# Scales of the Strassen pairs from sums of squares on ScalarE instead of largest weights on VectorE

## The reference

```python
def even_layer(x, norm_g, w_in, pool_w, pool_scale, conv_w, w_out):
    h = rms_norm(x, norm_g)
    proj = h @ w_in                          # 1024 x 3072: u_a, z_a, h_b, b_b, c_b, z_b
    ...
    y_a = pool_mixer(u_a, pool_w, pool_scale) * jax.nn.silu(z_a)      # windows 2, 4, 8, 16
    y_b = short_conv_mixer(h_b, b_b, c_b, conv_w) * jax.nn.silu(z_b)  # b * conv3(c * h)
    return x + jnp.concatenate([y_a, y_b], axis=-1) @ w_out

def odd_layer(x, cos, sin, norm_g, w_in, ...):
    h = rms_norm(x, norm_g)
    c_q, c_kv, k_rope, z = jnp.split(h @ w_in, ...)                   # 1024 x 2080
    ...                                                               # latent attention, 16 heads
    return x + (o * jax.nn.silu(z)) @ w_out                           # 1024 x 1024
```

## Time and profile before

| | |
|---|---|
| three runs | 961.5, 960.9, 961.76 us (median 961.5) |
| profiled execution, first to last instruction | 960.9 us |
| mean granted TensorE clock | 0.998 |
| PE busy | 947.5 us (99%) |
| DVE busy | 812.9 us (85%) |
| ACT busy | 575.2 us (60%) |
| POOL busy | 353.1 us (37%) |

### The profile page before, as it was taken

One profiled execution on the slowest core, in us unless ns is written; L12 is line 12 of the kernel. 1 busy time (PEld: TensorE's weight loads), 2 busy tenths in 40 slices (PEclk: granted clock), 3 DMA queues, 4 the chain that ended last, 5 costly groups with the idle time before them and its releaser, 6 DMA issues.

```text
span 960.9 us, 17257 instructions
## 1 busy us (share of the span) xinstructions
PE 947.5 (99%) x6406; PEld 671.3 (70%) x6406; DVE 812.9 (85%) x1410; ACT 575.2 (60%) x1076; POOL 353.1 (37%) x393
## 2 busy tenths in 40 slices
PE   9999999999999999999999999998999999999998
PEld 8788544444688887644457999996788888887443
DVE  5798899899865579988887899998999999998763
ACT  6443544424434454454646888866899989997230
POOL 0002233222000002235412577875652478894220
PEclk9999999999999999999999999999999999999999
DMA  9320422111054422332123264566676775460231
GB/s 305 45 61 23 110 77 56 44 45 45 1 175 155 152 67 67 107 112 58 31 72 111 89 205 150 204 181 176 119 163 145 171 150 122 82 179 2 88 110 65
DMA packets 165347, 103.74 MB, mean 108 GB/s; under 512 B 75272, under 2 KB 149520, under 8 KB 165008
## 3 DMA queue, kind: packets, MB, share of 16 engines
q1 hardware_dynamic: 159216, 102.25, 38.0%
q10 hardware_dynamic: 6048, 0.39, 0.5%
HBM read 56.48 MB, written 29.36 MB: 89 GB/s over the span
## 4 chain that ended last, share of the span: by engine, by line
PE 72%; DVE 19%; POOL 3%; issue 3%; ACT 2%; DVEq 0%; POOLq 0%; ACTq 0%
PE banks L111 19%; PE banks L113 19%; PE banks L112 19%; PE banks L2728 7%; PE banks L2746 2%; PE banks L2748 2%; PE banks L2747 2%; DVE heads_y L2480 1%; POOL heads_prod L2616 1%; DVE heads_x L2476 1%; DVE heads_x L2475 1%; DVE front_lt L1223 1%; DVE heads_ss L2522 1%; PE banks L2756 1%; DVE front_l L1223 1%
## 5 line engine op out<-in xcount | busy, mean ns | idle before, releaser
L2497 DVE TENSOR_TENSOR heads_pt_lo<-banks,heads_pt_hi 128x512 f16<-128x512 f32 (+2 forms) x192 | 102.1, 554 | 10.8 <-ACT heads_pt_hi L2360 7.8
L2360 ACT ACTIVATE heads_pt_hi<-banks 128x512 f16<-128x512 f32 (+2 forms) x192 | 89.1, 487 | 9.1 <-PE banks L2728 8.9
L2748 PE MATMUL banks<-heads_v,heads_pt_lo 128*128 128x64 f16 x576 | 71.1, 194 | 0.0
L2747 PE MATMUL banks<-heads_v,heads_pt_hi 128*128 128x64 f16 x576 | 71.0, 194 | 0.0
L2489 DVE CUSTOM_DVE_ANT_0 heads_probs_big<-banks,heads_mask,score_scale 128x1024 f32<-128x1024 f32 (+1 forms) x64 | 68.6, 1072 | 2.9 <-PE banks L113 2.7
L2746 PE MATMUL banks<-heads_v,heads_pt_hi 128*128 128x64 f16 x576 | 70.9, 194 | 0.0
L2728 PE MATMUL banks<-ident,heads_probs_big 128*128 128x128 f32 x416 | 69.5, 281 | 1.2 <-ACT heads_probs_big L2351 1.1
L2351 ACT ACTIVATE heads_probs_big<-heads_probs_big,heads_neg_max 128x1024 f32<-128x1024 f32 (+1 forms) x64 | 63.4, 990 | 8.8 <-DVE heads_neg_max L2489 7.7
L111 PE MATMUL banks<-heads_k_t,heads_q_t 96*128 96x512 f16 (+2 forms) x192 | 63.0, 328 | 1.0 <-DVE heads_neg_max L2489 1.0
L111 PE MATMUL banks<-front_act_hi,front_w_hi 128*128 128x512 f32 x160 | 63.8, 399 | 0.0
L113 PE MATMUL banks<-front_act_hi,front_w_lo 128*128 128x512 f32 x160 | 62.4, 390 | 0.0
(11 more groups left out here) (489 smaller groups left out, 3114.5 us busy)
## 6 DMA issues: line engine op xcount, KB each, us to landing
qk_scratch<-heads_y SPq DMA_DIRECT2D x22, 512.0 KB, 3.7
front_x<-in_x_t SPq DMA_DIRECT2D x16, 512.0 KB, 5.3
front_raw<-in_w_in_ab SPq DMA_DIRECT2D x14, 512.0 KB, 5.1
qk_scratch<-heads_last_y SPq DMA_DIRECT2D x10, 512.0 KB, 3.8
front_w<-in_w_out_ab SPq DMA_DIRECT2D x8, 512.0 KB, 3.9
x_scratch<-front_x SPq DMA_DIRECT2D x8, 512.0 KB, 3.9
v_scratch<-heads_v SPq DMA_DIRECT2D x32, 128.0 KB, 3.0
heads_v_st<-v_scratch SPq DMA_DIRECT2D x8, 512.0 KB, 5.2
```

Of the source, the lines that this page charges most:

```text
L2360: nc.scalar.activation(pt_hi[:, q % PIECES, :width], t_ps[:, banks[("piece", n, k)] % 3, :width], ACT.Copy).then_inc(pt_high, 1)
L2497: nc.vector.tensor_tensor(pt_lo[:, q % PIECES, :width], t_ps[:, banks[("piece", n, k)] % 3, :width], pt_hi[:, q % PIECES, :width], ALU.sub ...
L2747: nc.tensor.matmul(o_part, pt_hi[:, q % PIECES, blk], v2[e][:, j, VH:], start=False, stop=False)
L2748: last = nc.tensor.matmul(o_part, pt_lo[:, q % PIECES, blk], v2[e][:, j, :VH], start=False, stop=(j == i))
```

## The change

The sum of the largest weights becomes a sum of squares. `pair_norm` on ScalarE squares the 2048 weights of a partition and adds them up (Square with an accumulator output, the squares themselves go to a scratch place). The row sum on TensorE is the same matmul. `norm_scale` on VectorE then makes an approximate inverse square root, times 2 to the 13, by integer arithmetic on the float's bits, and a reciprocal: with the unscale, four operations in place of three. The order changes too:

- ScalarE: `pair_norm(p+1)` stands behind snapshot 1 of pair p (in pair 0 behind snapshot 2), for the even pairs ahead of the first tap. `pair_norm(0)` and `pair_norm(8)` stand ahead of pair 0 and pair 8, the output pairs' ones ahead of their forms.
- TensorE: the row sum is issued behind product 3 in place of 1 (pairs 1 to 7) or 2 (pairs 8 to 13); pair 0 and the output pairs stay as they were.
- VectorE: no peaks; `pair_scale` stands at the end of `pool_sums` and, in `conv`, behind the multiplication by b.

```diff
+def norm_scale(nc, link, total, size, scale):
+
+    top = float(0x5F3759DF + (13 << 23))
+    link(nc.vector.tensor_scalar(size, total, TINY, None, ALU.max))
+    link(nc.vector.tensor_scalar(scale.bitcast(I32), size.bitcast(I32), -0.5, top, ALU.mult, ALU.add))
+    link(nc.vector.reciprocal(size, scale))
...
+        def pair_norm(p):
+            raw_landed(act, p)
+            if p > 1:
+                act.wait_ge(row_spread, p - 1)
...
+            source = x[:, 0:CHUNKS, BANK:] if p == 0 else raw(p)[:].rearrange("p m (h k) c -> p (m h) (k c)", h=2)
+            nc.scalar.activation(dump[:], source, ACT.Square, accum_out=w_row[:, p % 2:p % 2 + 1]).then_inc(row_peak, 1)
...
                 snapshot(p, 1)
+                if p and p + 1 < PAIRED:
+                    pair_norm(p + 1)
                 if p and p % 2 == 0:
                     first_tap(g - 1)
...
                 snapshot(p, 2)
+                if p == 0:
+                    pair_norm(1)
...
                 snapshot(p, 1)
+                if not last_pair:
+                    pair_norm(p + 1)
                 if p == GATE_PAIRS - 1:
                     latent_high(2)
...
+            if n == OUT0 - 2:
+                pair_norm(0)
...
         high(ROPE0)
+        pair_norm(PAIRED)
         pair_forms(PAIRED, range(FORMS))
...
-            if p < PAIRED:
-                pair_scale(p)
             link(nc.vector.tensor_scalar(head[:, :win], count[:, :win], float(win), None, ALU.min))
...
             nc.vector.tensor_tensor(d_lo[:], other, f32(d_hi[:]), ALU.subtract).then_inc(d_ready, 1)
+            if p < PAIRED:
+                pair_scale(p)
...
             dve.sem_inc(ch_ready, 1)
-            if p < PAIRED:
-                pair_scale(p)
             dve.wait_ge(tapped, g + 1)
...
             dve.sem_inc(convolved, 1)
+            if p < PAIRED:
+                pair_scale(p)
...
-        def pair_peak(p):
-            raw_landed(dve, p)
...
-            nc.vector.tensor_reduce(w_row[:, p % 2:p % 2 + 1], x[:, 0:CHUNKS, BANK:] if p == 0 else
...
-            link(nc.vector.tensor_scalar(w_size[:, one], spread_ps(p), TINY, 2.0 ** -13, ALU.max, ALU.mult))
-            link(nc.vector.reciprocal(w_scale[:, one], w_size[:, one]))
+            norm_scale(nc, link, spread_ps(p), w_size[:, one], w_scale[:, one])
...
-                    if p + 1 < PAIRED and i == (1 if p else 4):
+                    if p + 1 < PAIRED and i == (3 if p else 4):
                         row_sum(p + 1)
...
-                    if p + 1 < ALL_PAIRS and i == 2:
+                    if p + 1 < ALL_PAIRS and i == 3:
                         row_sum(p + 1)
...
-    def peak(self, dve, q):
+    def pair_norm(self, act, q):
...
+                out.pair_norm(act, 0)
                 for c in range(2):
                     out.gate_high(act, NK - 2, c)
...
         for q in range(1, out.OUT_PAIRS):
+            out.pair_norm(act, q)
             out.forms_high(act, q)
...
-                out.peak(dve, 0)
...
-                out.peak(dve, q + 1)
```

More of the change, by code:

```diff
@@ L271, in front @@
     set_odd = [at(f"set_odd{i}", [P, 2, BANK], F16, odd_at[i]) for i in range(FORMS)]
+    norm_dump = at("norm_dump", [P, CHUNKS, BANK], F16, spare)
+    first_dump = at("first_dump", [P, CHUNKS, BANK], F16, w_place + 6 * ROW)
+    odd_dump = at("odd_dump", [P, CHUNKS, BANK], F16, arena)
     later_snap = [at(f"later_snap{n}", [P, BANK], F32, place) for n, place in enumerate(
@@ L724, in pair_forms @@
                                      scale=w_scale[:, p % 2:p % 2 + 1]).then_inc(form_high, 1)
+        def pair_norm(p):
[3 more added lines that the diff above has]
+            if p < PAIRED:
+                dump = norm_dump
+            elif p == PAIRED:
+                dump = first_dump
+            else:
+                if p == PAIRED + 1:
+                    act.wait_ge(act_low, RIGHT0 + SIX * CHUNKS)
+                dump = odd_dump if p % 2 else norm_dump
+            source = x[:, 0:CHUNKS, BANK:] if p == 0 else raw(p)[:].rearrange("p m (h k) c -> p (m h) (k c)", h=2)
+            nc.scalar.activation(dump[:], source, ACT.Square, accum_out=w_row[:, p % 2:p % 2 + 1]).then_inc(row_peak, 1)
         def snapshot(p, i):
@@ L1264, in later_paired @@
                 last_pair = p + 1 == ALL_PAIRS
-                if not last_pair:
-                    pair_peak(p + 1)
                 if p == PAIRED:
@@ L1338, in paired @@
             later_forms(1)
-            pair_peak(1)
             later_forms(2)
@@ L1342, in paired @@
                 g = p // 2
-                if 1 <= p < PAIRED - 1:
-                    pair_peak(p + 1)
                 if p % 2:
@@ L1402, in vector @@
                     first_forms(n - RING + 1)
-                if n == OUT0 - 3:
-                    pair_peak(0)
                 if n == OUT0 - 2:
@@ L1444, in vector @@
         low(ROPE0)
-        pair_peak(PAIRED)
         plain_gate(2)
@@ L1915, in t_form_low @@
                                      self.t_hl[:, f, 0, self.CHUNKS - 1], ALU.subtract).then_inc(self.t_low, 1)
-    def peak(self, dve, q):
+    def pair_norm(self, act, q):
         m = self.PLAIN + 2 * q
         for n in range(2):
-            dve.wait_ge(self.w_in[m + n], 32)
+            act.wait_ge(self.w_in[m + n], 32)
         if q == 0:
-            dve.wait_ge(self.joint.s_added, 4 * ALL_PAIRS + 4)
-        self.nc.vector.tensor_reduce(self.w_row[:, q:q + 1], self.w[:, m:m + 2].rearrange("p m k c -> p (m k c)"),
-                                     AX_X, ALU.max, apply_absolute_value=True).then_inc(self.joint.row_peak, 1)
+            act.wait_ge(self.joint.s_added, 4 * ALL_PAIRS + 4)
+        if q == self.OUT_PAIRS - 1:
+            act.wait_ge(self.t_low, self.form_base + 4)
+        dump = self.left[q][:, 0:2].rearrange("p i l k c -> p i l (k c)") if q else self.t_hl[:, 0:2, :, self.CHUNKS - 1]
+        self.nc.scalar.activation(dump, self.w[:, m:m + 2].rearrange("p m (h k) c -> p m h (k c)", h=2), ACT.Square,
+                                  accum_out=self.w_row[:, q:q + 1]).then_inc(self.joint.row_peak, 1)
     def row_sum(self, pe, q):
@@ L1935, in pair_scale @@
         dve.wait_ge(self.joint.row_spread, ALL_PAIRS + q + 1)
-        link(self.nc.vector.tensor_scalar(self.w_size[:, one], self.spread_ps(q), TINY, 2.0 ** -13, ALU.max, ALU.mult))
-        link(self.nc.vector.reciprocal(self.w_scale[:, one], self.w_size[:, one]))
+        norm_scale(self.nc, link, self.spread_ps(q), self.w_size[:, one], self.w_scale[:, one])
         link(self.nc.vector.tensor_tensor(self.unscale[:, one], self.w_size[:, one], self.r_unit, ALU.mult))
@@ L2580, in vector @@
             out.snapshot(dve, q, 0)
-            if more:
-                out.peak(dve, q + 1)
             out.snapshot(dve, q, 1)
```

4 lines of the change are left out of this document (removed).

## The result

The changed kernel takes **967.57 us** (median of five runs, 967.45 to 969.61), the kernel before 961.67 in the same comparison: ratio 1.0067, 95% interval 1.0055 to 1.0079. The forecast was 964.4 with a range of 961.0 to 966.7: the sign was right, the size was half of what came (+2.9 against +5.9), and the time lies above the range.

What follows compares the result with a forecast made beforehand. The prediction took TensorE as the bound, with 4.9 us lost in eight stalls. Its terms, 6.2 - 0.86 - 0.36 - 1.32 - 1.16 + 0.4 = +2.9 us on a median of 961.5, gave 964.4 us, range 961.0 to 966.7.

Steps and rivals of the forecast that it cites:

- The mechanism in the even pairs: Pairs 2, 4, 6: the square delays the tap and the scale lengthens VectorE's chain before product 6, +6.2 us for the three.
- it fits, by about 0.5 us: Odd pairs: VectorE's work after the late row sum, some 4.4 us, fits in the two products (5.2 us) until product 6.
- (a): Even pairs: ScalarE's square between snapshot 1 and the tap takes about 1.9 us and delays the multiply-adds by 1.05 us.
- (b): Even pairs: the scale, now four operations, stands on VectorE's chain behind the product with B, +0.97 us.
- (c): Pair 1: the row sum for pair 2, issued two products later, no longer waits for its operand, -0.86 us.
- (d): Pair 5: without the peak the running sums start earlier and the stall for quarter 1 goes, -0.36 us.
- (e): Pair 8: without its peak the gate is early enough, so the start and product 2 come in time, -1.32 us.
- (f): Pair 11: without the peak ahead of it quarter 1 is about in time, -1.16 us.
- (g): Pairs 10 to 13: ScalarE's crowding and the later row sum and scale cost +0.4 us, between 0 and 1.5.
- the third (more lands): Rival: snapshot 2 misses product 4, row sum late in odd pairs too, 0.3 us times 10 more, 967.5 us; chance 0.10.
- Rival 1: VectorE's load was the bound: without the peaks the eight TensorE stalls go, 957.0 us; chance 0.11.

Runs made afterwards that it cites:

- e1: The changed kernel with ScalarE's sum of squares ahead of snapshot 1 in pairs 2, 4 and 6, not behind it; 963.9 us.
- e3: The changed kernel plus a useless VectorE reduction of pair p+1's weights in pairs 1, 3 and 5, where the peak stood; 969.98 us.
- e5: The changed kernel with GpSimd's four sums of quarters for pairs 2 and 6 cut to one column each, output not the reference's; median 968.32 us.
- e4: The kernel before, with its own peak and three-operation scale, but the new late places of row sum and scale; 966.55 us.
- e6: The changed kernel with the old places of row sum and scale in pairs 1, 3, 5 and the square ahead of snapshot 0 there; 969.56 us.
- e2: The kernel before with only the engine changed: squares on ScalarE in its idle time, four-operation scale, old places for row sum and scale; 959.59 us.
- e11: The changed kernel run again unaltered, for the spread of its single times and the clock; 967.86 us.
- e8: e2 with the scale behind the multiplication by B and, in even pairs, an earlier pool map split, square and tap on ScalarE; 958.5 us.
- e10: The kernel before with only ScalarE's pool map split ahead of the previous pair's last quarter and the tap ahead of snapshot 1; 960.52 us.
- e9: e8 with VectorE's four key-table operations moved behind pair 11's last low forms; 957.56 us.
- e7: The changed kernel with the old places in pairs 8 to 13: square ahead of snapshot 1, row sum behind product 2; median 967.97 us.

## Why the prediction was wrong

The mechanism in the even pairs was right, to 0.3 us of 6.2. What failed is the gain set against it: the late places were taken as free in odd pairs ("it fits, by about 0.5 us"), and the peaks of pairs 5 and 11 as time that comes back in full. Term by term:

- **(a) the square: right.** 1.90 us, the next operation 1.89 behind its start (1.9 forecast). The tap, 184.46 before, plus the shift of 1.72 would be 186.18; it starts at 187.23, +1.05, the figure of the forecast. e1 shows that this counts in full (1.1 to 1.3 per pair).
- **(b) the scale on the chain: right.** It added 0.95 for 0.97, and quarter 1 of pair 4 came 2.00 us later relative to its pair. The three even pairs gave +5.87 for +6.2.
- **(c), (d) the odd pairs: the step that failed.** I had -0.86 and -0.36 and got +0.35 and +0.16, 1.7 us off. The stall at the row sum did go (0.88), but one of 1.23 came before product 6 of the same pair. Three things in "it fits, by about 0.5 us" were false. First, the scale does not start when the row sum is there (128.7 in pair 1) but when the running sums end (131.0). Second, taking the peak away hardly brings that end forward. Without it the sums run beside all of GpSimd's: they start 2.2 us earlier and are stretched by some 1.6 us more than with a reduction ahead of them (e3 starts them at 124.07 and the scale at 131.56, the changed kernel at 121.85 and 130.91); e5 shows that it is GpSimd. Third, in pair 1 another low part of 1.21 us stands between quarters 0 and 1, which I had not counted. So the late places cost in odd pairs too (e4, e6).
- **(e) pair 8: right**, -1.28 for -1.32.
- **(f) pair 11: failed in the same way.** I had -1.16 and got +0.22, 1.4 us off. Removing the peak gave only 0.2 (with the old places 1.00 remained of 1.20), since 1.8 us went into operations that now ran beside GpSimd's; and the late places in pair 10 added 0.42, a wait that I had looked for in pair 12 and not there.
- **(g)** +0.64 for +0.4, inside its bounds.

Sum of the misses: -0.3 + 1.7 + 1.4 + 0.2 = +3.0, the distance of 2.9 and 5.9. Of the rivals, the third (more lands) was the nearest: its time, 967.5, met the measured one by luck, while its "row sum comes late in odd pairs too" was right. Its price of 0.3 in ten pairs was not, since beside the even pairs only pairs 1, 5, 11 and 13 paid; and its own terms, 3.0 and the 1.1 up to the upper bound of (g), would have given 968.5. Rival 1 was wrong as a forecast for this change, yet e2 shows that the new engine is worth 2.4 us when row sum and scale keep their places. What I did not see is that the change is a gain and a loss that could be costed apart.

The clock, for which the sum held nothing, does not explain the median: three of the five runs had a mean of 0.998, like the kernel before, and the profiled one of them ran all its pairs at 2.4 GHz. The two long ones (0.996) fit a further stretch at half clock, as e11's profile shows one; they were not profiled themselves. The prediction read the mean of 0.998 as a clock that never fell behind the stalls it listed. That was so in the pairs, but the list left out the wait of 1.82 us in the attention, and behind that one the clock did fall (e11).

## What to carry to other kernels

Work taken off an engine is worth only what its removal uncovers: if it stood beside work of another engine that did not slow it, what follows may move up beside that work, be slowed by it, and the time does not come back. When an operation moves to another engine, put it where that engine waits (e2, e8), not ahead of a result that a third engine waits for, and keep small serial steps (a scale) off the end of a chain that has no slack. Before an engine is relieved, ask what starts its chain: here a 0.3 us split behind the wrong snapshot held up 12 us of VectorE's work, and moving it and the tap was worth 1.4 us with nothing else changed (e10).

## What the runs showed of the hardware

- Beside GpSimd's additions of 128x512 float32, VectorE's two-element operations took 0.93 to 1.12 us where they had to wait (0.16 without), a 128x1024 cast 1.73 (0.69) and four 128x128 products with two SBUF inputs 3.30 to 4.03 (1.26 in e9). GpSimd's additions themselves went from 1.27 to as much as 2.33. A reduction of 128x2048 took 2.28 beside them (pair 1) and with GpSimd idle (at 385.8 in the kernel before).
- After a stall of 2.34 us on a TensorE that was otherwise full, the granted clock fell in some executions from 1.00 to 0.50 (2.4 to 1.2 GHz), between 0.1 us before and 1.4 us after the restart, and rose again while the matmuls ran on without a hole, at a cost of some 1.7 us each time. Kernels with three such stalls (the changed kernel, e3, e5, e6, e7, e11) had a mean clock of 0.996 or less in 19 of 31 executions; those whose longest stall in the pairs was 1.81 or less (e1, e2, e4, e8, e9, e10) in none of 44.
- The length of the stall alone does not decide it: in the attention, where TensorE was less full, the clock fell behind a wait of 1.82 us in 9 of 13 profiled executions, the kernel before among them. What decides in a single execution stays open.
